# Each norm joined to the projection stage behind it in a two-layer hybrid block

## The chip, the cores and the metric

One Trainium2 chip, one of its cores. A core has TensorE (PE for its matmuls, PEld for its weight loads), VectorE (DVE), ScalarE (ACT), GpSimd (POOL) and SyncE (SP, which issues DMAs here). The metric is the device time of one execution in microseconds, lower is better; a version stands for the median of its runs.

## The reference, cut to what matters

Two layers, 512 latent tokens and 256 context tokens of width 1024. Each layer has two sublayers, and each begins with a layer norm and a modulation (a scale and a shift per channel), whose result goes at once into a wide projection:

```python
def _ln_plain(x):
    xf = x.astype(jnp.float32)
    mu = jnp.mean(xf, axis=-1, keepdims=True)
    var = jnp.mean(jnp.square(xf - mu), axis=-1, keepdims=True)
    return ((xf - mu) * lax.rsqrt(var + LN_EPS)).astype(x.dtype)

def _modulate(x, shift, scale):
    return _ln_plain(x) * (1.0 + scale) + shift
...
        cache, ctx_mix = _ctx_mixer(_modulate(xc, mod_c[0], mod_c[1]), lp, lam, lam_init, not last)
        lat_mix = _latent_mixer(_modulate(x, mod[0], mod[1]), lp, lam, lam_init, cache, cos, sin)
        x = _layernorm(alpha * x + mod[2] * lat_mix, ln1_g[i], ln1_b[i])
        x = _layernorm(alpha * x + mod[5] * _conv_ffn(_modulate(x, mod[3], mod[4]), lp), ln2_g[i], ln2_b[i])
```

The mixers multiply by `w_in` (the recurrent branch's 15 column tiles of it come first in the kernel), `_conv_ffn` multiplies by `ffn_up` (44 column tiles). The last layer's second sublayer works on the 512 latent tokens alone.

## The kernel before

The program is a row of stages. Each is one `stage(nc)` (L108): a block in which each engine runs its own list of instructions in order, with semaphores between them, and at whose end all engines meet at a barrier (L118, L122 in the rows) before the next stage's first instruction of any engine, DMAs included. So a stage cannot load its weights while the one before it runs.

`norm` (L300) is such a stage, and runs four times: before `rwkv_inputs` (L413) and before `ffn` (L1802) in each of the two layers. It works on `nt` token tiles of 128 tokens, 6 of them in the first three norms and 4 in the last. DVE takes the statistics (L318, L322), ACT the square root (L350), DVE the reciprocal and then the normalised tokens `xn`, one `tensor_scalar` for each token tile (L330). Then come eight channel tiles j of 128 channels: TensorE transposes `xn` into PSUM, `nt` transposes for a j (L344), ACT scales and shifts them into one of three slots of `h_f32` (L356), POOL rounds the slot to the fp32r number `h_hi` (L363), and DVE takes the rest, `h_lo` (L334). ACT waits for the `h_lo` three tiles back before it fills a slot again.

A projection, `fm_product` (L396), makes one column tile of 128 outputs for all tokens: for each of the 8 channel tiles k, three products, `w_hi` by `h_hi`, `w_hi` by `h_lo` and `w_lo` by `h_hi`. With 768 tokens each of them is two matmuls (512 and 256 columns), so that a product of one column tile has 48 matmuls; with 512 tokens 24. Its weights come by one DMA of 512 KB (`load_weights`, L379), are rounded by ACT (`split_hi`, L387), and the rest is taken by POOL (`split_lo`, L393). Three raw slots and two split slots hold them: the split for column tile n waits until product n-2 is done. In `rwkv_inputs` ACT copies a finished product out (L575), in `ffn` it does at L1834.

The order is the one written out by hand in these functions; no scheduler changes it.

## Time and profile before

| | us |
|---|---|
| median of 3 runs | 4311.81 (4307.54 to 4319.73) |
| the profiled execution | 4310.86 |
| its span | 4308.5 |
| PE busy | 3610.2 (84% of the span) |
| DVE, ACT, POOL busy | 1549.0, 968.3, 1032.3 |
| granted TensorE clock, mean | 0.928 |

The page has one section that bears on this change, the costliest groups, where the matmuls at L402 (these projections) show a wait for POOL's `w_lo`. The rest is in the trace itself: the list of waits, the timeline around a norm (each row: start, length, engine, line, operation, out<-in, form, count, and in brackets the idle time before it with what ended it), and the windows view, whose columns are the stretch and its length, then the busy time of PE, PEld, DVE, ACT and POOL in it, each with its count (or of one engine alone), the granted clock, the DMA share and GB/s. Clock 0.50 is 1.2 GHz and 1.00 is 2.4 GHz. SPq is SP's queue; a DMA row there is the issue, not the transfer.

### The profile page before, as it was taken

The numbers are of one execution on the slowest core, as the hardware profiler recorded it, in microseconds if no ns is written. First come the engines' busy times: TensorE is split into PE (matmuls) and PEld (weight loads), VectorE is DVE, ScalarE is ACT, GpSimd is POOL, SyncE is SP. The second block draws the span as 40 slices with busy tenths as digits, with TensorE's granted clock in tenths as the row PEclk, the third lists the DMA queues.
The fourth block names the chain that finished last, engine by engine and source line by source line (L and its number), as shares of the span: only waits on it lengthen the run. The fifth ranks groups of instructions, "written<-read, shape, count | busy, mean of one in ns | idle before, by whom it ended". The sixth has DMA issues, their size and how long they took to land. (4 is left out here: it accounts for less than half of the span.)

```text
span 4308.5 us, 80797 instructions
## 1 busy us (share of the span) xinstructions
PE 3610.2 (84%) x36124; PEld 2680.1 (62%) x36124; DVE 1549.0 (36%) x2266; ACT 968.3 (22%) x1743; POOL 1032.3 (24%) x633
## 2 busy tenths in 40 slices
PE   4979999996587888699999497999996687669987
PEld 3658888885355663588734276888774355438843
DVE  2243443332576153311201524444542672331102
ACT  2322212211255120222200142222221342203300
POOL 1222222223232110222200222232232331214401
PEclk8989999998799999799999798999998898879998
DMA  5643333322111231122153054333432102313321
GB/s 196 219 154 105 101 110 101 105 77 109 38 45 46 75 98 78 54 64 64 42 183 138 31 159 132 90 101 108 118 100 86 54 30 94 121 59 93 98 98 39
DMA packets 432706, 410.71 MB, mean 95 GB/s; under 512 B 14244, under 2 KB 367706, under 8 KB 425450
## 3 DMA queue, kind: packets, MB, share of 16 engines
q1 hardware_dynamic: 430778, 396.77, 29.3%
q10 hardware_dynamic: 1584, 8.78, 0.5%
q8 instruction: 285, 4.67, 0.5%
q14 instruction: 59, 0.48, 0.0%
HBM read 325.15 MB, written 80.35 MB: 94 GB/s over the span
## 5 line engine op out<-in xcount | busy, mean ns | idle before, releaser
L799 PE MATMUL ps<-I-280_h_hi,I-1976_w_hi 128*128 128x256 f32 (+1 forms) x832 | 298.4, 359 | 26.9 <-POOL I-1977_w_lo L393 16.0
L799 PE MATMUL ps<-I-280_h_hi,I-1977_w_lo 128*128 128x256 f32 (+1 forms) x832 | 282.2, 339 | 0.1
L799 PE MATMUL ps<-I-281_h_lo,I-1976_w_hi 128*128 128x256 f32 (+1 forms) x832 | 282.1, 339 | 0.0
L1917 PE MATMUL ps<-I-21320_w_down,I-18160_hf 128*128 128x512 f32 x528 | 234.0, 599 | 9.2 <-DMA I-21320_w_down<-in_ffn_down 9.2
L799 PE MATMUL ps<-I-22069_h_hi,I-23484_w_hi 128*128 128x512 f32 (+1 forms) x544 | 215.3, 396 | 19.8 <-POOL I-23485_w_lo L393 14.2
L799 PE MATMUL ps<-I-22070_h_lo,I-23484_w_hi 128*128 128x512 f32 (+1 forms) x544 | 202.5, 372 | 0.5 <-issue 0.5
L799 PE MATMUL ps<-I-22069_h_hi,I-23485_w_lo 128*128 128x512 f32 (+1 forms) x544 | 202.7, 373 | 0.0
L402 PE MATMUL ps<-I-18161_h_hi,I-18370_w_hi 128*128 128x512 f32 x704 | 180.2, 337 | 15.8 <-POOL I-18371_w_lo L393 15.8
L1917 PEld LDWEIGHTS ps<-I-21320_w_down,I-18160_hf 128*128 128x128 f32 x528 | 99.2, 191 | 143.2 <-issue 133.2
L778 POOL CAST I-1976_w_hi<-I-1975_w_raw 128x1024 fp32r<-128x1024 f32 x52 | 56.3, 1082 | 545.7 <-PE ps L799 530.4
L799 PEld LDWEIGHTS ps<-I-280_h_hi,I-1976_w_hi 128*128 128x128 f32 x832 | 157.2, 189 | 43.9 <-POOL I-1977_w_lo L393 16.8
L402 PE MATMUL ps<-I-18162_h_lo,I-18370_w_hi 128*128 128x512 f32 x704 | 180.0, 337 | 0.0
L402 PE MATMUL ps<-I-18161_h_hi,I-18371_w_lo 128*128 128x512 f32 x704 | 179.9, 337 | 0.0
L799 PEld LDWEIGHTS ps<-I-281_h_lo,I-1976_w_hi 128*128 128x128 f32 x832 | 157.9, 190 | 19.2 <-issue 5.0
L799 PEld LDWEIGHTS ps<-I-280_h_hi,I-1977_w_lo 128*128 128x128 f32 x832 | 157.4, 189 | 19.1 <-issue 0.3
L393 POOL TENSOR_TENSOR I-18371_w_lo<-I-18369_w_raw,I-18370_w_hi 128x1024 fp32r<-128x1024 f32 x44 | 105.7, 2403 | 260.5 <-ACT I-18370_w_hi L387 260.5
L778 POOL CAST I-23484_w_hi<-I-23483_w_raw 128x1024 fp32r<-128x1024 f32 x52 | 60.1, 1155 | 444.6 <-PE ps L799 419.1
L1917 PE MATMUL ps<-I-39044_w_down,I-37054_hf 128*128 128x512 f32 x352 | 153.6, 599 | 9.2 <-DMA I-39044_w_down<-in_ffn_down 9.2
L402 PE MATMUL ps<-I-37055_h_hi,I-37230_w_hi 128*128 128x512 f32 x352 | 138.1, 392 | 13.8 <-POOL I-37231_w_lo L393 13.8
L393 POOL TENSOR_TENSOR I-37231_w_lo<-I-37229_w_raw,I-37230_w_hi 128x1024 fp32r<-128x1024 f32 x44 | 105.6, 2401 | 138.2 <-ACT I-37230_w_hi L387 138.2
L402 PE MATMUL ps<-I-37056_h_lo,I-37230_w_hi 128*128 128x512 f32 x352 | 137.8, 392 | 0.0
L402 PE MATMUL ps<-I-37055_h_hi,I-37231_w_lo 128*128 128x512 f32 x352 | 137.7, 391 | 0.0
(837 smaller groups left out, 8202.8 us busy)
## 6 DMA issues: line engine op xcount, KB each, us to landing
I-1975_w_raw<-in_w_in SPq DMA_DIRECT2D x52, 512.0 KB, 5.6
I-23483_w_raw<-in_w_in SPq DMA_DIRECT2D x52, 512.0 KB, 5.1
I-21324_ada_w<-in_ada_w SPq DMA_DIRECT2D x24, 1024.0 KB, 4.9
I-18369_w_raw<-in_ffn_up SPq DMA_DIRECT2D x44, 512.0 KB, 3.9
I-37229_w_raw<-in_ffn_up SPq DMA_DIRECT2D x44, 512.0 KB, 3.8
proj_d<-I-1978_result SPq DMA_DIRECT2D x52, 384.0 KB, 2.8
I-502_ada_w<-in_ada_w SPq DMA_DIRECT2D x16, 1024.0 KB, 5.8
I-21320_w_down<-in_ffn_down SPq DMA_DIRECT2D x22, 512.0 KB, 5.9
```

The costliest lines, as they stand in the source:

```text
L393: eng.tensor_tensor(rings[2][:, n % n_split, 0:kt, :], rings[0][:, n % n_raw, 0:kt, :], rings[1][:, n % n_split, 0:kt, :].bitcast(F32), AL ...
L402: m = pe.matmul(dst[:, at:at + n], w[wi][:, k, :], a[ai][:, k, at:at + n], start=k == 0 and i == 0, stop=k == kt - 1 and i == 2)
L778: pool.tensor_copy(rings[1][:, s % 2, :, :], rings[0][:, s % 3, :, :]).then_inc(sem("w_hi"), 1)
L799: m = pe.matmul(bank(6 + i % 2, n_c), w[:, k, :], hv[:, k, c0:c0 + n_c], start=k == 0 and v == 0, stop=k == KT - 1 and v == 2)
L1917: m = pe.matmul(bank(t), hf[:, g * KG + k, t * P:(t + 1) * P], ring[:, i % SL, k, :], start=g == 0 and k == 0, stop=g == NG - 1 and k == K ...
```

## The change

`norm` is no stage of its own any more. It is called inside the block of `rwkv_inputs` or `ffn` and lays its instructions ahead of theirs on each engine, so that the barrier between the two is gone; SP has no part in the norm, and its first instruction in the block is the load of the first weights. Three things move with it.

First, the weights of column tile 0 are split by ACT ahead of the square root and by POOL ahead of the eight casts; column tiles 1 and on follow behind the norm. Second, the product of column tile 0 waits for `h_lo` tile by tile (`n_lo`), not for the whole norm; its result lies in PSUM banks 0 and 1, and the transposes have three pairs of banks, not four, so that they wait for ACT one tile sooner. Third, one in three of the `xn` tiles goes to ACT, with a bias that a new small DVE instruction makes from mean and reciprocal (`neg_mean`); DVE has 4 of 6 tiles, or 3 of 4. The buffers `xn` and `h_f32` share memory with ones that the stage fills later. The number of matmuls is the same.

```diff
-            with ExitStack() as sc, stage(nc) as (block, sem):
...
+        def norm(sc, block, sem, l, i_shift, i_scale, nt, h, xn, hf, rings):
...
+            by_dve = [t for t in range(nt) if t % 3 != 2]
+            by_act = [t for t in range(nt) if t % 3 == 2]
...
+                dve.wait_ge(sem("n_rstd"), 1)
+                dve.scalar_tensor_tensor(nb[:, 0:nt], mv[:, 0:nt, 0], -1.0, rs[:, 0:nt], ALU.mult, ALU.mult).then_inc(sem("n_nb"), 1)
+                for t in by_dve:
+                    dve.tensor_scalar(xn[:, t, :], x[:, t, :], mv[:, t, 0:1], rs[:, t:t + 1],
+                                      ALU.subtract, ALU.mult).then_inc(sem("n_xn"), 1)
...
+                pe.wait_ge(sem("n_xn"), len(by_dve))
+                pe.wait_ge(sem("n_xa"), len(by_act))
+                for j in range(KT):
+                    if j >= 3:
+                        pe.wait_ge(sem("n_h"), j - 2)
+                    for t in range(nt):
+                        m = pe.transpose(bank(2 + 2 * (j % 3), P, t * P), xn[:, t, j * P:(j + 1) * P], ident[:, :])
...
+                split_hi(act, sem, rings, 0)
+                act.wait_ge(sem("n_var"), 1)
+                act.activation(rs[:, 0:nt], rs[:, 0:nt], ACT.Sqrt).then_inc(sem("n_std"), 1)
+                act.wait_ge(sem("n_nb"), 1)
+                for t in by_act:
+                    act.activation(xn[:, t, :], x[:, t, :], ACT.Identity, bias=nb[:, t:t + 1], scale=rs[:, t:t + 1]).then_inc(sem("n_xa"), 1)
...
+                split_lo(pool, sem, rings, 0)
+                for j in range(KT):
+                    pool.wait_ge(sem("n_h"), j + 1)
+                    pool.tensor_copy(h[0][:, j, 0:n_tok], hf[:, j % 3, 0:n_tok]).then_inc(sem("n_hi"), 1)
...
+                        if s == 1:
+                            pe.wait_ge(sem("n_h"), KT)
                         if s >= 4:
                             pe.wait_ge(sem("hf"), s // 2 - 1)
-                        fm_product(pe, p_of(s), slot(rings, s), h, range(KT), KT, seqs).then_inc(sem("w_used"), 1)
+                        for k in range(KT):
+                            if s == 0:
+                                pe.wait_ge(sem("n_lo"), k + 1)
+                            m = fm_product(pe, p_of(s), slot(rings, s), h, (k,), KT, seqs)
+                        m.then_inc(sem("w_used"), 1)
...
-                    for s in range(3):
+                    for s in range(1, 3):
                         split_hi(act, sem, rings, s)
...
-                    for s in range(2 * FT):
+                    for s in range(1, 2 * FT):
                         split_lo(pool, sem, rings, s)
-                    norm(l, 0, 1, NT, h)
-                    norm(l, 3, 4, LT if last else NT, h)
```

In `rwkv_inputs` the product is cut in the same way, and its first `split_hi` and `split_lo` move too.

Three places in the order of the instructions show this. The first is POOL at the first norm, before (`I-284_h_f` is a slot of `h_f32`, `w_raw`, `w_hi` and `w_lo` are the weights, L118 to L122 the barrier):

```order
L359 UNCONDITIONAL_BRANCH
L363 CAST I-280_h_hi<-I-284_h_f 128x768 x8
L118 UNCONDITIONAL_BRANCH
L121 ISA
L592 UNCONDITIONAL_BRANCH
L393 ISA
L393 TENSOR_TENSOR I-501_w_lo<-I-499_w_raw,I-500_w_hi 128x1024 x15
```

and in the change (the slots of `h_f32` are now `rv_raw`):

```order
L409 UNCONDITIONAL_BRANCH
L328 ISA
L328 TENSOR_TENSOR I-295_w_lo<-I-293_w_raw,I-294_w_hi 128x1024
L414 CAST I-280_h_hi<-I-286_rv_raw 128x768 x8
L608 UNCONDITIONAL_BRANCH
L328 TENSOR_TENSOR I-295_w_lo<-I-293_w_raw,I-294_w_hi 128x1024 x14
```

One subtraction for the weights has moved ahead of the casts, and 14 stand behind them with no barrier between. The second place is ACT at the last norm, the one of 4 token tiles, in the change:

```order
L393 UNCONDITIONAL_BRANCH
L322 ACTIVATE I-37007_w_hi<-I-37006_w_raw 128x1024
L397 ACTIVATE I-37013_rstd<-I-37013_rstd 128x4
L400 ACTIVATE I-37002_hf<-I-49_x,I-37014_neg_mean,I-37013_rstd 128x1024
L406 ACTIVATE I-37010_h_f<-ps,I-64_mod 128x512 x8
L1853 UNCONDITIONAL_BRANCH
L322 ACTIVATE I-37007_w_hi<-I-37006_w_raw 128x1024 x2
```

The rounding of the first weights now stands ahead of the square root (L397), one `xn` tile (L400) behind it, and the rounding for column tile 1 comes right after the last of the eight tiles. The third is TensorE at the first norm, in the change:

```order
L390 MATMUL ps<-I-50_ident,I-283_k_and_kk 128x128 x48
L503 UNCONDITIONAL_BRANCH
L337 MATMUL ps<-I-280_h_hi,I-294_w_hi 128x512
L337 MATMUL ps<-I-280_h_hi,I-294_w_hi 128x256
L337 MATMUL ps<-I-281_h_lo,I-294_w_hi 128x512
```

against before:

```order
L344 MATMUL ps<-I-50_ident,I-283_xn 128x128 x48
L118 UNCONDITIONAL_BRANCH
L495 UNCONDITIONAL_BRANCH
L402 MATMUL ps<-I-280_h_hi,I-500_w_hi 128x512
L402 MATMUL ps<-I-280_h_hi,I-500_w_hi 128x256
```

All 48 transposes still stand ahead of the first product; what is gone between the two is the barrier.

## Rows read from the trace of the kernel before

**Rows 1.** List of waits of PE from 40 to 260 us: waiter, releaser, us in total, times, longest.

```profile
PE ps L402 <- POOL I-501_w_lo L393: 17.0, 1, 17.0
```

**Rows 2.** Timeline from the first norm to the end of the first product.

```profile
41.09 1.28 ACT L350 ACT_TABLE_LOAD   x1 [1.97 <-PEq L122]
41.13 7.22 DVE L318 BATCH_NORM_STATS2 I-285_stats<-I-49_x 128x6 f32<-128x512 f32 x12 [0.86 <-PEq L122]
...
49.52 4.43 DVE L330 TENSOR_SCALAR I-283_xn<-I-49_x,I-286_mean_var,I-287_rstd 128x1024 f32<-128x1024 f32 x6
54.01 7.78 PE L344 MATMUL ps<-I-50_ident,I-283_xn 128*128 128x128 f32 x48 [14.18 <-DVE I-283_xn L330]
...
65.77 1.23 ACT L356 ACTIVATE I-284_h_f<-ps,I-63_mod 128x512 f32<-128x512 f32 x2 [0.30 <-DVE I-281_h_lo L334]
67.06 0.83 POOL L363 CAST I-280_h_hi<-I-284_h_f 128x768 fp32r<-128x768 f32 x1 [0.70 <-ACT I-284_h_f L356]
68.62 0.94 DVE L334 TENSOR_TENSOR I-281_h_lo<-I-284_h_f,I-280_h_hi 128x768 fp32r<-128x768 f32 x1
70.72 0.37 SPq L379 DMA_DIRECT2D I-499_w_raw<-in_w_in  x1
...
75.22 1.06 ACT L387 ACTIVATE I-500_w_hi<-I-499_w_raw 128x1024 fp32r<-128x1024 f32 x1 [8.22 <-DMA I-499_w_raw<-in_w_in]
...
76.36 2.34 POOL L393 TENSOR_TENSOR I-501_w_lo<-I-499_w_raw,I-500_w_hi 128x1024 fp32r<-128x1024 f32 x1 [8.47 <-ACT I-500_w_hi L387]
...
78.75 1.00 PE L402 MATMUL ps<-I-280_h_hi,I-500_w_hi 128*128 128x512 f32 x2 [16.96 <-POOL I-501_w_lo L393]
...
89.25 0.90 ACT L575 ACTIVATE I-489_wa_raw<-ps,I-57_mu_own 128x768 f32<-128x768 f32 x1 [6.37 <-PE ps L402]
```

**Rows 3.** Windows view: the first product behind each of the four norms.

```profile
78.75:89.20 10.45, 10.45 (x52) 8.88 (x56) 0.00 (x0) 1.06 (x1) 2.40 (x1) 0.81 1.00 334
1770.05:1781.25 11.20, 11.20 (x49) 9.69 (x50) 0.00 (x0) 0.00 (x0) 2.28 (x1) 0.75 0.32 94
2481.18:2491.90 10.72, 10.72 (x49) 9.30 (x50) 0.00 (x0) 1.06 (x1) 2.37 (x1) 0.79 0.43 118
3870.07:3878.10 8.03, 8.03 (x25) 6.42 (x26) 0.00 (x0) 0.00 (x0) 2.26 (x1) 0.70 0.45 131
```

**Rows 4.** Timeline: last h_lo and end of product 0, second and third norm.

```profile
1760.57 0.94 DVE L334 TENSOR_TENSOR I-18162_h_lo<-I-18165_h_f,I-18161_h_hi 128x768 fp32r<-128x768 f32 x1
...
1781.33 1.06 ACT L387 ACTIVATE I-18370_w_hi<-I-18369_w_raw 128x1024 fp32r<-128x1024 f32 x1 [11.95 <-PE ps L402]
...
2472.04 0.94 DVE L334 TENSOR_TENSOR I-22070_h_lo<-I-22073_h_f,I-22069_h_hi 128x768 fp32r<-128x768 f32 x1
...
2491.94 0.90 ACT L575 ACTIVATE I-22278_wa_raw<-ps,I-58_mu_own 128x768 f32<-128x768 f32 x1 [9.63 <-PE ps L402]
```

**Rows 5.** Timeline of the fourth norm, of 4 token tiles.

```profile
3841.82 4.85 DVE L318 BATCH_NORM_STATS2 I-37060_stats<-I-49_x 128x6 f32<-128x512 f32 x8 [2.93 <-PEq L122]
...
3847.47 0.18 DVE L327 RECIPROCAL I-37062_rstd<-I-37062_rstd 128x4 f32<-128x4 f32 x1 [0.27 <-ACT I-37062_rstd L350]
...
3860.94 0.69 DVE L334 TENSOR_TENSOR I-37056_h_lo<-I-37059_h_f,I-37055_h_hi 128x512 fp32r<-128x512 f32 x1 [0.51 <-POOL I-37055_h_hi L363]
...
3866.53 1.06 ACT L387 ACTIVATE I-37230_w_hi<-I-37229_w_raw 128x1024 fp32r<-128x1024 f32 x1 [6.84 <-DMA I-37229_w_raw<-in_ffn_up]
...
3878.15 1.06 ACT L387 ACTIVATE I-37230_w_hi<-I-37229_w_raw 128x1024 fp32r<-128x1024 f32 x1 [8.75 <-PE ps L402]
```

**Rows 6.** Timeline: the same DVE instruction alone, and beside a POOL instruction.

```profile
1696.37 0.81 DVE L1780 TENSOR_SCALAR I-49_x<-I-49_x,I-17981_mean_var,I-17982_rstd 128x1024 f32<-128x1024 f32 x1
...
1726.00 2.34 POOL L1794 TENSOR_TENSOR I-49_x<-I-49_x,I-17866_ln_b 128x1024 f32<-128x1024 f32 x1 [11.38 <-DVE I-49_x L1782]
1726.03 2.86 DVE L1780 TENSOR_SCALAR I-49_x<-I-49_x,I-17981_mean_var,I-17982_rstd 128x1024 f32<-128x1024 f32 x1
```

**Rows 7.** Windows view, from 2.2 us behind the first norm's transposes.

```profile
64.00:70.00 6.00, 0.00 (x0) 0.00 (x0) 5.56 (x5) 2.46 (x4) 2.48 (x3) 0.64 0.00 0
```

More of the change, by code:

```diff
@@ L420, in rwkv_inputs @@
             with ExitStack() as s2, stage(nc) as (block, sem):
-                kf = sb(s2, "k_raw", [P, CTILES, TOK])
+                kfk = sb(s2, "k_and_kk", [P, 2, CTILES, TOK])
+                kf, kk = kfk[:, 0], kfk[:, 1]
                 wa = sb(s2, "wa_raw", [P, 2, TOK])
@@ L431, in rwkv_inputs @@
                 rings = weight_rings(s2, 3, 2)
+                xn = kfk[:, :, :, :].rearrange("p a t n -> p (a t n)").rearrange("p (t d) -> p t d", t=NT)
+                norm(s2, block, sem, l, 0, 1, NT, h, xn, rv, rings)
                 src = A["w_in"][l].rearrange("(k p) n -> p k n", p=P)
@@ L533, in _ @@
                         pe.wait_ge(sem("w_lo"), n + 1)
+                        if n == 1:
+                            pe.wait_ge(sem("n_h"), KT)
                         if n >= 2:
                             pe.wait_ge(sem("shifted"), n - 1)
-                        fm_product(pe, p_of(n), slot(rings, n), h, range(4), KT, seqs(mains[n]))
+                        for k in range(4):
+                            if n == 0:
+                                pe.wait_ge(sem("n_lo"), k + 1)
+                            fm_product(pe, p_of(n), slot(rings, n), h, (k,), KT, seqs(mains[n]))
                         beside(2 * n)
-                        fm_product(pe, p_of(n), slot(rings, n), h, range(4, KT), KT, seqs(mains[n])).then_inc(sem("w_used"), 1)
+                        for k in range(4, KT):
+                            if n == 0:
+                                pe.wait_ge(sem("n_lo"), k + 1)
+                            m = fm_product(pe, p_of(n), slot(rings, n), h, (k,), KT, seqs(mains[n]))
+                        m.then_inc(sem("w_used"), 1)
                         beside(2 * n + 1)
@@ L593, in _ @@
                 def _(pool):
-                    for n in range(N):
+                    for n in range(1, N):
                         split_lo(pool, sem, rings, n)
@@ L1809, in ffn @@
                 cv = sb(s2, "conv", [P, 2, TOK])
+                xn = hf[:, FT - KT:FT, :].rearrange("p j n -> p (j n)").rearrange("p (t d) -> p t d", d=D_MODEL)
+                h3 = sb(s2, "h_f32", [P, 3, TOK])
+                norm(s2, block, sem, l, 3, 4, nt, h, xn, h3, rings)
                 src = A["ffn_up"][l].rearrange("(k p) n -> p k n", p=P)
```

102 lines of the change are left out of this document (43 added, 59 removed).

## The prediction

> **What bounds the kernel now.** I first read the list of waits of TensorE for the stretch of the first norm and the projections behind it. Its longest entry is one wait of 17.0 us for POOL's `w_lo` [rows 1]. The timeline shows what lies in it [rows 2]. The transposes end at 54.01 + 7.78 = 61.8. The last `h_lo` ends at 68.62 + 0.94 = 69.56. Only then, behind the barrier, does SP issue the load of the first weights (70.72); they are there at 75.22, ACT rounds them for 1.06 us, POOL takes the rest for 2.34 us, and the first matmul starts at 78.75. So 9.2 us pass between the end of the norm and the first product, in which ACT and POOL together have 3.4 us of work, and all of it serves a load that depends on nothing the norm makes. The product of column tile 0 then runs from 78.75 until ACT may copy it out at 89.25.
>
> That pattern occurs four times. In the second and third norm the last `h_lo` ends at 1761.51 and 2472.98, and product 0 has ended at 1781.3 and 2491.9 [rows 4]; in the fourth it is 3861.63 and 3878.1 [rows 3, 5]. The windows view says what product 0 is made of: 10.45 us at a mean granted clock of 0.81 [rows 3]. 10.45 x 0.81 = 8.46 us is what it needs at 2.4 GHz, so 2.0 us are lost because the clock stood at 1.2 GHz when it began. The others give 8.40, 8.47 and 5.62 us, and losses of 2.8, 2.25 and 2.4; the four losses come to 9.4 us. One channel tile of eight thus costs 1.06 us at 2.4 GHz, and 0.70 us with 512 tokens. Behind product 0 TensorE is the bound of these stages: [rows 1] gives the wait for `w_lo` as one single time up to 260 us, so whatever product 0 ends earlier, the stage ends earlier.
>
> **The change part by part.** I work in the times of the trace of before, and ask when product 0 ends.
>
> The gap. The load is now issued when the block starts, near 41.1. In [rows 2] it took 75.22 - 70.72 = 4.5 us, so it lands at 45.6; ACT rounds until 46.7, then loads its table (1.28 us, until 48.0). The statistics end at 41.13 + 7.22 = 48.35 and the root is wanted about 0.7 us before `xn` starts at 49.52, so ACT is free 0.8 us before. POOL's subtraction runs from 46.8 to 49.1, and it had nothing to do then. SP's other loads and the three large ones of `ada_w` come earlier too, and wait for nothing new. The cost of these moved steps in the three norms with 6 token tiles is taken as nothing; the DVE statistics cover it. If POOL and the statistics hinder one another, it costs up to 2.86 - 0.81 = 2.05 us a norm, what a DVE instruction lost beside POOL in [rows 6]; below nothing it cannot be, as the norm is not made shorter by it. No row shows statistics beside POOL, so both ends stay in the range, and I take nothing because the subtraction is over by 49.1, before the long `xn` instructions begin.
>
> `xn`. Six instructions take 4.43 us on DVE [rows 2], 0.74 each. Four take 2.95, and the new small one costs about as much as the reciprocal, 0.18 us [rows 5], with its semaphore 0.22. ACT's two tiles are the size of a weight rounding, 1.06 us each: 2.1 us, hidden beside DVE's 2.95. Gain 4.43 - 2.95 - 0.22 = 1.25 us in each of the first three norms.
>
> The fourth norm has less cover. Its statistics take 4.85 us from 3841.82 [rows 5]. The weights land at 3841.8 + 4.5 = 3846.3, ACT has rounded them at 3847.4, and POOL works from 3847.5 to 3849.8. DVE's reciprocal is done at 3847.65, so the small instruction and three `xn` tiles fall right onto POOL. [rows 6] show the price: the same form on DVE takes 0.81 us alone and 2.86 us when it starts 0.03 us behind a POOL instruction of 2.34, so it stands still until POOL ends. I let DVE wait until 3849.8: 3849.8 + 0.22 + 3 x 0.74 = 3852.25, where before it was done at about 3847.68 + 4 x 0.74 = 3850.65. This norm loses 1.6 us at `xn`; the bounds are that and a gain of 0.5.
>
> Product 0, fed tile by tile. TensorE runs in order, so it starts only behind all transposes. Those wait for ACT one tile sooner, but the last ACT tile began at 65.77, 4 us behind the transposes' end, so the eighth transpose has room. From 61.8 seven tiles of 1.06 us need 7.4 us, until 69.2; the seventh `h_lo` ends at 68.62, where the eighth begins [rows 2], so tile seven ends at 69.2 to 69.7 and TensorE keeps up with DVE. The eighth decides. ACT is done with its last tile at 65.77 + 1.23 = 67.0, rounds column tile 1 until 68.1, and POOL, whose last cast ended at 67.89, asks for its subtraction at about 68.15, while DVE is in the seventh `h_lo`. When that ends at 68.62, POOL has been waiting longest. I let it go first, as in [rows 6]: the eighth `h_lo` starts 2.34 us late. Product 0 ends at 68.62 + 2.34 + 0.94 + 0.1 + 1.06 = 73.06 (0.1 for two semaphores), less 1.25: 71.8. Product 1 finds its `w_lo` ready at 68.62 + 2.34 = 70.96, less 1.25.
>
> The Trainium skill (SBUF — State Buffer, section "Who interferes with whom") says that DVE and GpSimd share a pair of ports as a lock: a DVE instruction with two SBUF inputs, or in a two-port mode, and a GpSimd instruction that reads SBUF shut each other out for the whole length, and whichever issues first goes first; one with a single input outside those modes is not hindered. By that rule the tail goes to POOL and the statistics pay nothing, which is the sum below; were nothing shared, the sum would be 4.1 us at the tails and 2.1 us at the fourth `xn` better. [rows 6] agree with the lock, with 2.86 us against 0.81.
>
> The sum, as the end of product 0 before less the end now:
> - first norm: 89.2 - 71.8 = 17.4
> - second: 1781.3 - (1760.57 + 4.44 - 1.25 = 1763.75) = 17.5
> - third: 2491.9 - (2472.04 + 4.44 - 1.25 = 2475.25) = 16.7
> - fourth: 3878.1 - (3860.94 + 2.34 + 0.69 + 0.1 + 0.70 + 1.6 = 3866.4) = 11.7
>
> Together 63.3 us. The jump from the norm's list to the stage's on each engine is new and not in the trace; a barrier with two jumps and SP's first issue takes 70.72 - 69.56 = 1.16 us, so one jump costs 0 to 1.16. On TensorE it is hidden, since it comes seven tiles before the deciding one; on ACT it would only turn the tail over, which is the first rival. The profiled execution was 4310.86, 1 us from the median 4311.81: 4310.86 - 63.3 = 4247.6.
>
> **The rivals.**
> (a) DVE goes first at the tails. If ACT's jump costs more than 0.5 us, POOL asks behind 68.62 and the eighth `h_lo` is not held. Then `w_lo` of column tile 1 decides: 69.56 + 2.34 + 0.05 = 71.95 for product 1's start, against 73.06. That is 1.1 us better, 3 x 1.1 + 0.8 = 4.1 in all: 4243.5. Against it, the margin of 0.5 us is most of what a barrier costs.
> (b) The clock is not kept. [rows 7] show it at a mean of 0.64 from 64 to 70 us, which is 2.4 GHz for 0.28 x 6 = 1.7 us, until 65.7: it fell 3.9 us behind the last transpose. The idle time I leave TensorE before tile eight is 73.06 - 1.06 - 69.7 = 2.3 us, shorter. A clock at 1.2 GHz during product 0 alone is nearly free (61.8 + 11.2 = 73.0, no later than DVE allows). But if it falls at the tail, product 1 pays what product 0 paid before, 9.4 us in all: 4257.
> (c) The weights' steps hinder the first three norms as well: 3 x 2.05 = 6.2 us, 4253.8.
> (d) The change doesn't overlap as it says, and product 0 runs wholly behind the last `h_lo`: it loses seven tiles each, 3 x 7.4 + 4.9 = 27.1 us, 4274.7. The order of the instructions speaks against it.
> (e) Slower than before. ACT now waits for the first weights ahead of the square root, and everything in the norm hangs on that root. Each microsecond that the load takes beyond about 5.3 us (4.5 and the 0.8 of slack) delays the norm by one. To lose 13 us overall each load would have to be late by (63.3 + 13) / 4 = 19 us, so to take 24 us against the 4.5 of [rows 2]. No row speaks for that.
>
> **How the numbers follow.** Forecast 0.52, (a) 0.16, (b) 0.14, (c) 0.09, (d) 0.04; 0.04 for a gain that is partly given back in the stages, most of it still faster, and 0.01 for (e). The range runs from (a), 4243.5, and from (b), 4257, each with some 4 us more for the jump, the fourth norm and the spread of three runs: 4239 to 4261. It leaves out (d), (e) and the rest, about 0.1, and a mixture of (b) and (c). A measurement of this kernel can tell about 0.3%, 13 us, from no change: faster by more 0.97, within 0.02, slower 0.01.
>
> **What would show it.** In the trace of the changed kernel the first `w_raw` load is issued with the statistics, `w_lo` ends before `xn` starts, and TensorE's wait behind the transposes is no longer 17 us but several short ones for DVE's `h_lo`, the last near 2.3 us. At the tail a POOL subtraction of 2.34 us stands between the seventh and eighth `h_lo`. `xn` ends 1.25 us sooner in three norms and later in the fourth. I am wrong if the clock is at 0.5 in product 1, if ACT's table load or root comes late, or if the stages behind product 0 have grown.

## The result and the profile after the change

The changed kernel takes 4256.28 us (median of 4 runs, 4247.08 to 4261.71), beside 4312.68 for the kernel before (4 runs, 4307.54 to 4319.73). The medians lie 56.4 us apart. The ratio is 0.9863, with a 95% interval of 0.9848 to 0.9878: faster by 1.4%, clear of the noise. The forecast was 4247.6 in a range of 4239 to 4261. The profiled run took 4255.81 us with a span of 4254.0, where the kernel before had 4310.86 and 4308.5.

First the list of waits of TensorE for the changed kernel, in the stretch of [rows 1] (waiter, releaser, us in total, times, longest):

```profile
PE ps L390 <- DVE I-283_k_and_kk L375: 12.8, 1, 12.8
...
PE ps L337 <- DVE I-281_h_lo L379: 1.7, 1, 1.7
```

The 17.0 us for `w_lo` are gone. What is left is the wait ahead of the transposes (L390) for the `xn` tiles (their buffer bears the name `k_and_kk` here), which was there before too (14.18 in [rows 2]), and 1.7 us for one `h_lo`. The timeline of the first norm answers to [rows 2] (start, length, engine and line, operation, in brackets the idle time before it and its releaser):

```profile
41.26 0.37 SPq L314 DMA_DIRECT2D I-293_w_raw<-in_w_in  x1
41.30 7.22 DVE L362 BATCH_NORM_STATS2 I-296_stats<-I-49_x 128x6 f32<-128x512 f32 x12 [0.86 <-PEq L122]
...
45.38 1.06 ACT L322 ACTIVATE I-294_w_hi<-I-293_w_raw 128x1024 fp32r<-128x1024 f32 x1 [6.09 <-DMA I-293_w_raw<-in_w_in]
...
46.46 1.28 ACT L397 ACT_TABLE_LOAD   x1
46.52 2.34 POOL L328 TENSOR_TENSOR I-295_w_lo<-I-293_w_raw,I-294_w_hi 128x1024 fp32r<-128x1024 f32 x1 [45.60 <-ACT I-294_w_hi L322]
...
49.23 0.21 ACT L397 ACTIVATE I-298_rstd<-I-298_rstd 128x6 f32<-128x6 f32 x1 [1.49 <-DVE I-298_rstd L369]
...
61.27 0.60 PE L337 MATMUL ps<-I-280_h_hi,I-294_w_hi 128*128 128x512 f32 x2
...
66.83 2.90 POOL L328 TENSOR_TENSOR I-295_w_lo<-I-293_w_raw,I-294_w_hi 128x1024 fp32r<-128x1024 f32 x1
...
70.60 0.62 PE L337 MATMUL ps<-I-280_h_hi,I-294_w_hi 128*128 128x512 f32 x2 [1.71 <-DVE I-281_h_lo L379]
...
71.96 0.90 ACT L591 ACTIVATE I-284_wa_raw<-ps,I-57_mu_own 128x768 f32<-128x768 f32 x1 [5.21 <-PE ps L337]
```

The load is issued with the statistics and both splits are over by 48.9, before `xn` starts. ACT stands idle for 1.49 us ahead of the square root, so the weights' steps cost the norm nothing. The first matmul of product 0 starts at 61.27, right behind the transposes, and product 0 is copied out at 71.96 instead of 89.25. The windows view gives product 0 at each of the four places, as [rows 3] did (window, its length, busy us of PE, PEld, DVE, ACT and POOL, then the granted clock):

```profile
61.20:72.00 10.80, 9.09 (x55) 7.52 (x57) 9.35 (x6) 4.69 (x8) 6.32 (x5) 1.00 0.00 0
1733.50:1744.40 10.90, 9.77 (x56) 8.31 (x55) 8.39 (x5) 5.03 (x9) 5.43 (x4) 1.00 0.17 47
2433.50:2444.30 10.80, 9.09 (x53) 7.72 (x52) 9.32 (x6) 4.73 (x8) 6.30 (x5) 1.00 0.08 22
3815.00:3823.40 8.40, 6.57 (x29) 5.12 (x28) 5.53 (x4) 3.41 (x5) 5.24 (x5) 1.00 0.17 49
```

The granted clock is 1.00 (2.4 GHz) at all four, where it was 0.81, 0.75, 0.79 and 0.70. Product 0 is not much shorter than before. Its first seven channel tiles run through right behind the transposes, and ahead of the eighth TensorE waits for the last `h_lo`, 1.71, 1.13, 1.71 and 1.83 us at the four places, where before it ran at 1.2 GHz behind the norm.

**Where the time went.** I cut each execution into five parts: four places, each from the start of a norm's statistics to the start of ACT's copy of product 0 (in the two ffn ACT rounds another column tile ahead of that copy, before and after alike); the first layer's ffn, from its first copy to its last (22 copies, each of two column tiles); and the rest. All are read off the traces, and the parts sum to the span up to rounding.

```
us                         four places                 sum     ffn of layer 0   rest     span
before                     48.1  49.2  47.4  37.3     182.0   348.4            3778.1   4308.5
after                      30.7  31.7  30.6  25.6     118.6   355.1            3780.3   4254.0
```

The four places gained 63.4 us. The first ffn lost 6.7 and the rest 2.2, which leaves 54.5.

The 6.7 us are not a wait. The windows view has TensorE busy all through the stage and the granted clock at 1.00, in the kernel before and then in the changed one:

```profile
1790.00:2130.00 340.00, 340.00 (x1963) 297.39 (x1962) 61.06 (x100) 76.82 (x82) 98.59 (x41) 1.00 0.21 59
```

```profile
1750.00:2095.00 345.00, 345.00 (x1954) 299.22 (x1954) 61.07 (x100) 77.20 (x82) 98.26 (x41) 1.00 0.20 59
```

But the matmuls take a little longer. The groups by form, first of the kernel before from 1800 to 2130 us, then of the changed one from 1765 to 2095 (busy us, mean ns of one):

```profile
L402 PE MATMUL ps<-I-18161_h_hi,I-18370_w_hi 128*128 128x512 f32 x318 | 125.1, 394 | 0.0
L402 PE MATMUL ps<-I-18162_h_lo,I-18370_w_hi 128*128 128x512 f32 x318 | 125.1, 394 | 0.0
...
L402 PE MATMUL ps<-I-18162_h_lo,I-18370_w_hi 128*128 128x256 f32 x317 | 87.8, 277 | 0.0
```

```profile
L337 PE MATMUL ps<-I-18144_h_lo,I-18147_w_hi 128*128 128x512 f32 x312 | 125.8, 403 | 0.0
L337 PE MATMUL ps<-I-18143_h_hi,I-18148_w_lo 128*128 128x512 f32 x312 | 124.2, 398 | 0.0
L337 PE MATMUL ps<-I-18143_h_hi,I-18147_w_hi 128*128 128x512 f32 x311 | 122.9, 395 | 0.0
L337 PE MATMUL ps<-I-18144_h_lo,I-18147_w_hi 128*128 128x256 f32 x312 | 88.6, 284 | 0.0
```

The lengths overlap, since a matmul starts before the one ahead of it ends. A 128x512 matmul with `h_lo` takes 403 ns instead of 394, one of 256 columns 284 instead of 277; the other two products have 398 and 395 with 512 columns. So the loss is not spread evenly: one of the three products of each channel tile takes most of it. In the second execution of this kernel (again, below) that one was `h_hi` by `w_hi`. The six matmuls of a channel tile start 1040 ns after those of the last one in before (1043 and 1037 in turn), and 1060 in after, from the second product to the last without a drift. I call these the 1040 and the 1060 pace. From the first to the last of ACT's copies there are 336 channel tiles: 336 x 0.02 = 6.7 us.

### The profile page after: what moved, and what is told of

Its sections match the earlier page's. It is cut to its first block and busy times, and to the rows that moved or that the text cites. A ratio compares the mean times of both kernels' runs of the same rounds, so it can differ in the third digit from the quotient of the medians.

```text
span 4254.0 us, 80709 instructions
## 1 busy us (share of the span) xinstructions
PE 3614.4 (85%) x36124; PEld 2680.1 (63%) x36124; DVE 1555.2 (37%) x2263; ACT 976.0 (23%) x1750; POOL 1032.5 (24%) x633
## 5 line engine op out<-in xcount | busy, mean ns | idle before, releaser
L815 PE MATMUL ps<-I-280_h_hi,I-1958_w_hi 128*128 128x256 f32 (+1 forms) x832 | 299.6, 360 | 20.5 <-POOL I-1959_w_lo L328 15.0
L815 PE MATMUL ps<-I-281_h_lo,I-1958_w_hi 128*128 128x256 f32 (+1 forms) x832 | 283.2, 340 | 3.2 <-issue 3.2
L815 PE MATMUL ps<-I-280_h_hi,I-1959_w_lo 128*128 128x256 f32 (+1 forms) x832 | 283.4, 341 | 0.0
L1942 PE MATMUL ps<-I-21286_w_down,I-18142_hf 128*128 128x512 f32 x528 | 234.1, 600 | 9.1 <-DMA I-21286_w_down<-in_ffn_down 9.1
L815 PE MATMUL ps<-I-22035_h_hi,I-23432_w_hi 128*128 128x512 f32 (+1 forms) x544 | 215.8, 397 | 19.1 <-POOL I-23433_w_lo L328 15.2
L815 PE MATMUL ps<-I-22036_h_lo,I-23432_w_hi 128*128 128x512 f32 (+1 forms) x544 | 202.9, 373 | 0.0
L815 PE MATMUL ps<-I-22035_h_hi,I-23433_w_lo 128*128 128x512 f32 (+1 forms) x544 | 202.8, 373 | 0.0
L337 PE MATMUL ps<-I-18144_h_lo,I-18147_w_hi 128*128 128x512 f32 x704 | 184.7, 343 | 0.0
L337 PE MATMUL ps<-I-18143_h_hi,I-18147_w_hi 128*128 128x512 f32 x704 | 181.0, 338 | 1.1 <-DVE I-18144_h_lo L379 1.1
L337 PE MATMUL ps<-I-18143_h_hi,I-18148_w_lo 128*128 128x512 f32 x704 | 180.8, 338 | 0.0
L337 PE MATMUL ps<-I-37003_h_hi,I-37007_w_hi 128*128 128x512 f32 x352 | 137.2, 390 | 1.8 <-DVE I-37004_h_lo L379 1.8
L337 PE MATMUL ps<-I-37003_h_hi,I-37008_w_lo 128*128 128x512 f32 x352 | 137.0, 389 | 0.0
```

Of the source, the lines that this page charges most:

```text
L337: m = pe.matmul(dst[:, at:at + n], w[wi][:, k, :], a[ai][:, k, at:at + n], start=k == 0 and i == 0, stop=k == kt - 1 and i == 2)
L815: m = pe.matmul(bank(6 + i % 2, n_c), w[:, k, :], hv[:, k, c0:c0 + n_c], start=k == 0 and v == 0, stop=k == KT - 1 and v == 2)
L1942: m = pe.matmul(bank(t), hf[:, g * KG + k, t * P:(t + 1) * P], ring[:, i % SL, k, :], start=g == 0 and k == 0, stop=g == NG - 1 and k == K ...
```

## The experiments

Each is compared with the unchanged second run of the changed kernel or with the kernel before, part by part. All stand in one table, in us; "pace" is that of a channel tile in the first ffn, whose copies span 348.4 us at 1040 and 355.1 at 1060.

```
                           four places                 sum     pace, ns   rest     span
before                     48.1  49.2  47.4  37.3     182.0    1040      3778.1   4308.5
after                      30.7  31.7  30.6  25.6     118.6    1060      3780.3   4254.0
again                      30.7  31.7  30.7  25.0     117.9    1060      3781.6   4254.6
no_tile_feed               40.4  40.3  40.1  31.4     152.2    1040      3767.7   4268.3
late_split                 38.5  39.9  39.7  30.1     148.1    1040      3776.3   4272.8
second_split_early         29.2  30.1  29.2  23.2     111.7    1040      3785.2   4245.3
second_split_early_again   29.2  30.1  28.7  23.7     111.7    1040      3777.8   4237.9
merge_alone                41.3  42.8  41.2  30.8     156.1    1060      3778.7   4289.9
xn_all_dve                 32.3  33.1  32.0  26.0     123.4    1040      3774.2   4246.0
xn_all_dve_again           32.0  33.1  32.9  25.5     123.6    1060      3780.9   4259.6
late_load                  37.9  38.4  37.7  30.5     144.6    1060      3778.6   4278.3
hold_in_product0           29.3  31.0  29.2  23.3     112.8    1060      3779.6   4247.5
hold_again                 28.7  30.9  29.2  23.7     112.5    1060      3772.9   4240.5
hold_before_product1       28.7  30.3  29.2  23.7     111.9    1060      3782.9   4249.9
```

The places repeat within 0.9 us each and 0.7 in their sum; the rest goes from 3767.7 to 3785.2. No experiment edits anything in it (in two executions a late fall of the clock reaches into it, as told under (b) below). Most of the spread lies in the two layers' long stretches from product 0 to the norm ahead of the ffn (1635.8 to 1646.0 and 1346.4 to 1356.4 us). So a mechanism is read at its places, and a whole time alone settles nothing under some 10 us.

**again.** The changed kernel, nothing edited.

> The changed kernel once more. The four places gained 63.3 us in its first trace, as in the sum of the prediction, but the span fell by 54.5 only: 6.8 us went in the first layer's feed-forward projection, where a column tile took 16.91 / 2 us where before it took 16.59 / 2, with no wait of TensorE. Theory A (the rate of these matmuls varies from one execution to the next, with no tie to the change): the pace there differs from 16.91 for a pair in some of the traces of this call. Theory B (the change slows them): 16.91 again in each kernel that keeps its instructions. Time: 4250 to 4260.

4253.74 us, ratio 0.9848 (0.9833 to 0.9863), the places within 0.7 us in sum, and the same 1060 pace, which either theory allows.

**no_tile_feed.** Product 0 waits for all eight `h_lo`:

```
-                                pe.wait_ge(sem("n_lo"), k + 1)
+                                pe.wait_ge(sem("n_lo"), KT)
```

> Product 0 of each projection waits for all eight h_lo tiles, not tile by tile; all else as in the changed kernel. Theory: product 0 then starts at the last h_lo (70.55 us at the first norm) behind 9 us of idle TensorE, so that the clock has fallen, and takes as long as before the change, 10.45, 11.2, 10.7 and 8.0 us: it ends 9.2, 9.8, 9.4 and 7.0 us later than in the changed kernel, 35.4 us in all (4256 + 35 = 4291). Rival 1 (the clock holds): 7.4, 7.4, 7.4, 4.9, so 27 us. Rival 2 (the feed is worth nothing, since the early weights are what counts): within 5 us of the changed kernel.

4285.43 us, ratio 0.9924 (0.9907 to 0.994). The places lose 33.6 us against after, near the 35.4 of the theory, and the clock was lost: the windows view grants 0.50 over the first 3 us of product 0 in the second and third norm.

**late_split.** The split of the first weights stands behind the norm's own instructions on ACT and on POOL:

```
             def _(act):
-                split_hi(act, sem, rings, 0)
...
                     m.then_inc(sem("n_h"), 1)
+                split_hi(act, sem, rings, 0)
...
             def _(pool):
-                split_lo(pool, sem, rings, 0)
...
+                split_lo(pool, sem, rings, 0)
```

> The split of column tile 0's weights goes behind the norm's instructions on ACT and POOL; its load stays early, the feed tile by tile stays. Theory: POOL ends it at 69.75 at the first norm, TensorE has been idle for 8 us, product 0 runs cold and ends near 80.2 where the changed kernel has 71.9: 8.4, 8.9 and 8.5 us later in the first three norms; in the fourth 4.3, because POOL no longer stands in the way of DVE's small instructions there (2.2 us). 30 us in all, 4286. Rival (the load alone is what had to be early, 5.6 us of the 9.2 us gap): about 3.4 us a norm, 14 in all.

4272.77 us, ratio 0.9892 (0.9877 to 0.9906), and 29.5 us lost at the places, with 30 expected. The whole time came out 13 us under the 4286 expected: the profiled execution had the 1040 pace (6.7 us) and 4 us less in the rest than after. The timeline of its second norm shows the way:

```profile
1745.86 5.92 POOL L328 TENSOR_TENSOR I-18148_w_lo<-I-18146_w_raw,I-18147_w_hi 128x1024 fp32r<-128x1024 f32 x2
1748.78 0.50 PEld L337 LDWEIGHTS ps<-I-18143_h_hi,I-18147_w_hi 128*128 128x128 f32 x2 [7.78 <-POOL I-18148_w_lo L328]
1748.79 1.01 PE L337 MATMUL ps<-I-18143_h_hi,I-18147_w_hi 128*128 128x512 f32 x2 [7.55 <-POOL I-18148_w_lo L328]
```

POOL makes the first `w_lo` only behind its last cast, TensorE waits 7.55 us for it, and the clock is lost again: over 1745 to 1754 us the windows view grants 0.56, and two matmuls take 1.01 us where the changed kernel's take 0.60. Feeding tile by tile brings little without the early split, since product 0 needs `w_lo` in its first channel tile.

**merge_alone.** Both edits above, and all of `xn` on DVE; what stays is the single block with the early load.

> What is left of the change when its three parts are taken out: the norm still shares its block with the projection and the weights are still loaded at its start, but they are split behind the norm, product 0 waits for all of h_lo, and DVE makes all xn tiles. Theory: the barrier and the load (5.7 us of the 9.2 us gap) are gone, the split of 3.4 us is half hidden by the last h_lo tiles, product 0 runs cold as before: 6.9, 6.1, 5.8 and 6.2 us sooner than in the kernel before, 25 in all, 4290. Rival (the parts are not additive, each removes the same idle time): 40 us or more sooner.

4290.08 us, ratio 0.9922 (0.99 to 0.9944). The places gain 26.0 us on before: the load of 4.5 us and the barrier are hidden. Of the other 156.1 - 118.6 = 37.5 us, `xn` is 4.9 if it is worth here what xn_all_dve shows in the changed kernel (no run tests that), so tile feed and early split together are 32.6, not 33.6 + 29.5. With neither of them the places would come to 156.1 - 4.9 = 151.2; with the feed alone (late_split) they have 148.1, with the early split alone (no_tile_feed) 152.2. The two are one edit in two halves.

**xn_all_dve.** All token tiles of the norm on DVE (a list `by_dve` of all tiles and an empty `by_act`, and without the small instruction L373 for ACT's bias).

> The changed kernel with all xn tiles on DVE and without the small neg_mean instruction. Theory: product 0 ends 1.25 us later in the first three norms and 0.5 us later in the fourth, 4.3 us in all: 4259. Rival (ACT's share is worth nothing, since the transposes wait for something else): within 1 us at each place. If the pace of the second norm's projection goes back from 1060 to 1040 ns for a channel tile, 6.9 us come back and the time is 4252; this theory says nothing on that.

4263.07 us, ratio 0.9865 (0.984 to 0.989); 4.8 us lost at the places, and 5.0 in its second execution, with 4.3 expected.

**late_load.** SP issues the first weights only when the statistics are done:

```
+            if late and n == 0:
+                sp.wait_ge(sem("n_var"), 1)
```

> SP holds back the load of column tile 0 until DVE has the variances, about 8 us into the block (5.5 in the fourth norm); all else as in the changed kernel. This tests the rival in which ACT's wait for the weights ahead of the square root holds the norm. Theory: the root is late by what the load is late beyond the slack of 1.5 to 2.7 us seen in the changed trace: 6.4 us at the first norm (4.2 landing, 1.06 rounding, 1.28 table), 5.3 at the second and third, and POOL's subtraction then falls onto DVE's xn and costs up to 2 us more: 8, 7, 7 and 5 us, 27 in all, 4283. Other theory (ACT's place in the order is harmless, since TensorE waits for h_lo anyway): under 5 us.

4285.11 us, ratio 0.9922 (0.9906 to 0.9939); 25.9 us lost at the places, with 27 expected. Its first norm's timeline:

```profile
49.43 0.37 SPq L316 DMA_DIRECT2D I-293_w_raw<-in_w_in  x1
...
53.80 1.06 ACT L324 ACTIVATE I-294_w_hi<-I-293_w_raw 128x1024 fp32r<-128x1024 f32 x1 [14.31 <-DMA I-293_w_raw<-in_w_in]
...
54.88 1.28 ACT L399 ACT_TABLE_LOAD   x1
...
56.17 0.21 ACT L399 ACTIVATE I-298_rstd<-I-298_rstd 128x6 f32<-128x6 f32 x1
56.41 0.19 DVE L373 RECIPROCAL I-298_rstd<-I-298_rstd 128x6 f32<-128x6 f32 x1 [7.01 <-ACT I-298_rstd L399]
56.64 0.66 DVE L375 SCALAR_TENSOR_TENSOR I-299_neg_mean<-I-297_mean_var,I-298_rstd 128x6 f32<-128x6 f32 x1
```

The statistics start at 41.51 here. Counted from them, the load was issued 8.0 us later than in after and took 0.2 us more to be used; less the slack of 1.5 us that makes 6.7, and the root came 6.7 us later (14.66 us behind the start of the statistics against 7.93). The small instruction of L375 took 0.5 us more beside POOL, and this place lost 7.2. So at this place a late load costs what exceeds the slack of 1.5 us, one for one, as the rival on the slower side had it. Even a load 8 us later in three norms and 5.4 in the fourth leaves the kernel faster than before.

**second_split_early.** The split of column tile 1 is taken away from the tail of the norm: ACT does its half behind its `xn` tiles, POOL its half ahead of the casts, behind DVE's `xn`:

```
                 split_lo(pool, sem, rings, 0)
+                pool.wait_ge(sem("n_xn"), len(by_dve))
+                split_lo(pool, sem, rings, 1)
```

(ACT gets `split_hi(act, sem, rings, 1)` behind its `xn` loop, and the stage's own loops begin one column tile later.)

> Column tile 1 is also split ahead of the casts: by ACT behind its xn tiles, by POOL as soon as DVE has finished xn, while both engines wait for the first transposes. Theory: nothing stands between the seventh and the eighth h_lo any more, so that DVE's last one takes 0.94 us, not 3.1, and product 0 ends 1.9, 1.4, 1.9 and 1.8 us sooner than in the changed kernel; product 1 finds its weights ready. 7 us faster, 4249. Rival (the subtraction of 2.34 us merely moves the hold-up to the first cast): within 2 us of the changed kernel, and the first h_hi cast starts later by up to 2 us.

> second_split_early unchanged, a second time, in more rounds: its ratio to the kernel before was 0.9829 and that of after 0.9848 beside it, 6.4 to 8 us apart, of which 6.8 was counted at the four places (1.3 to 2.3 us at each) and 6.9 more would lie in the first ffn if its pace stays at 16.59 us for two products. Both would make 13.7 us under after, about 4240 to 4243; the four places alone make about 4247. Expected 4245, ratio 0.983 (0.981 to 0.985), pace 16.59, the places at 29.2, 30.1, 29.2 and 23.2 us.

4245.64 us, ratio 0.9829 (0.9814 to 0.9843); the second time 4250.28 and 0.9851 (0.983 to 0.9872), 5 us above the 4245 expected. The places gain 6.9 us on after in either execution. The timelines say why; first the tail of the second norm in after, then where the same split went in second_split_early:

```profile
1735.72 6.18 DVE L379 TENSOR_TENSOR I-18144_h_lo<-I-18150_h_f,I-18143_h_hi 128x768 fp32r<-128x768 f32 x3
...
1737.18 0.84 POOL L414 CAST I-18143_h_hi<-I-18150_h_f 128x768 fp32r<-128x768 f32 x1 [0.67 <-ACT I-18150_h_f L406]
1738.15 2.93 POOL L328 TENSOR_TENSOR I-18148_w_lo<-I-18146_w_raw,I-18147_w_hi 128x1024 fp32r<-128x1024 f32 x1
...
1741.95 0.62 PE L337 MATMUL ps<-I-18143_h_hi,I-18147_w_hi 128*128 128x512 f32 x2 [1.13 <-DVE I-18144_h_lo L379]
```

```profile
1725.58 2.36 POOL L328 TENSOR_TENSOR I-18149_w_lo<-I-18147_w_raw,I-18148_w_hi 128x1024 fp32r<-128x1024 f32 x1 [4.21 <-ACT I-18148_w_hi L322]
1726.60 2.51 ACT L407 ACTIVATE I-18151_h_f<-ps,I-63_mod 128x512 f32<-128x512 f32 x4 [1.17 <-PE ps L390]
1727.90 0.82 POOL L417 CAST I-18144_h_hi<-I-18151_h_f 128x768 fp32r<-128x768 f32 x1
```

In the one it stands between DVE and its last `h_lo`; in the other it fills the time in which the first transposes run and POOL has nothing to cast. By whole times it lies 8 us under again, beside which it was measured, with intervals that overlap, and the second time its ratio is no better than that of again (0.9851 and 0.9848). So whole times do not show that it is better; the places do, by 6.9 us twice.

With the tail gone TensorE decides these places. Product 0 runs through, and what is left to differ is a wait in the transposes for ACT to empty one of the three pairs of banks: of 1.0 to 1.1 us where the place has 29.2, and absent where it has 28.7 (first and third norm of these two and the hold kernels; one with 0.86 us has 29.3). In after such a wait (1.08 us, second norm) costs nothing, since DVE decides there.

**The pace: hold_in_product0, hold_again, hold_before_product1, xn_all_dve_again.** The changed kernel stops TensorE for 1.1 us inside product 0 (L337 above), and runs at 1060 from there; before and second_split_early have no such stop and run at 1040. Theory A: the stop makes the pace. The hold kernels are second_split_early with three more DVE instructions and a wait for them on TensorE, in layer 0's ffn alone, in hold_in_product0 (and hold_again, the same kernel) ahead of the eighth channel tile:

```
+                            if s == 0 and k == KT - 1 and not last:
+                                pe.wait_ge(sem("hold"), 1)
```

In hold_before_product1 the wait stands under `if s == 1`, ahead of product 1.

> The kernel with the second split early, and in the first layer's feed-forward stage three more DVE instructions of 0.6 us behind the last h_lo, for which TensorE waits ahead of the eighth channel tile of product 0 (they change nothing in the data). In the changed kernel TensorE stood still for 1.1 us at this place and then needed 1060 ns for each channel tile until the end of the stage, 43 products; with the second split early it did not stand still and needed 1040. Theory (a stop of TensorE inside product 0 sets the slower pace): 1060 again in this stage, 7 us more, 4252. Rival (the pace comes from something else, such as when product 1 begins against POOL or ACT): 1040, 4246.

> hold_in_product0 unchanged, a second time. If the pace of the first ffn's matmuls belongs to the program (the instants at which TensorE starts and stops in it), it is 16.91 us for two products again; if it is drawn at each execution, it may be 16.59. after and its repeat both had 16.91, which is one pair; this is a second. Four places 29.3, 31.0, 29.2, 23.3 us as the first time, each within 0.3.

> The kernel of hold_in_product0 with its wait moved: in the ffn of layer 0 TensorE waits for the three extra 0.6 us VectorE instructions (which multiply three h_lo tiles by 1.0 and change no data) ahead of product 1 instead of ahead of the last channel tile of product 0. The question is the pace of that stage's matmuls, which was 16.59 us for each two products in before and 16.91 in after. Theory A (a stop inside product 0 brings the slow pace) expects 16.59 here, since product 0 runs through and the stop lies between two products; theory B (the pace is picked anew at any restart, by something that no row shows) allows either. merge_alone, with 16.91 and no stop inside product 0, already speaks against A. The four places should stay at 29.2, 30 to 31, 29.2 and 23.2 us from the statistics to the copy out of product 0; the span is 4240 to 4250 with 16.59 and 7 us more with 16.91.

> xn_all_dve unchanged, a second time: it has a stop inside product 0 of the first ffn and still ran at 16.59 us for two products. A pace that belongs to the program gives 16.59 again; a drawn one gives 16.91 at about even odds, and then no cause is to be looked for in the kernel's text. Four places 32.3, 33.1, 32.1 and 26.1 us, each within 0.3.

hold_in_product0 had the 1060 pace (4249.29 us), as A wants; so had hold_again (4242.25) and hold_before_product1 (4251.68), and merge_alone without any stop inside product 0. The intervals between the last matmuls (`w_lo` by `h_hi`, 256 columns) of successive channel tiles overturn A. The first seven lie inside product 0, a bar, then come those of product 1 (ns, in the first ffn):

```
before                 1920 1900 1047 1042 1038 1042 1038 | 1042 1038 ...
after                  1040 1040 1040 1040 1040 1040 2465 | 1060 1060 ...
xn_all_dve             1040 1040 1040 1040 1040 1116 3037 | 1040 1040 ...
xn_all_dve_again       1038 1042 1038 1042 1038 1126 3065 | 1060 1060 ...
late_load              1060 1060 1060 1060 1060 1060 2326 | 1060 1060 ...
hold_in_product0       1060 1060 1060 1060 1060 1060 1718 | 1060 1060 ...
hold_before_product1   1060 1060 1060 1060 1060 1060 1060 | 1060 1060 ...
second_split_early     1040 1040 1040 1040 1040 1040 1040 | 1040 1040 ...
```

The places of the two repeats missed their expected 0.3 us at times: hold_again had 28.7 for 29.3 in the first norm and 23.7 for 23.3 in the fourth, xn_all_dve_again 32.9 for 32.1 in the third (its clock fell there) and 25.5 for 26.1 in the fourth.

In the hold kernels TensorE had the 1060 pace from the second tile on, before it ever came to the added wait. The wait was also short: 0.4 us in hold_in_product0 and hold_again, and in hold_before_product1 it never held TensorE. There the three added instructions (L1898) were over at 1744.69, and ACT, which waits for the end of product 0, went on only at 1745.57:

```profile
1743.19 1.50 DVE L1898 TENSOR_SCALAR I-18151_h_f<-I-18151_h_f 128x768 f32<-128x768 f32 x3
1745.57 1.06 ACT L322 ACTIVATE I-18148_w_hi<-I-18147_w_raw 128x1024 fp32r<-128x1024 f32 x1 [4.98 <-PE ps L337]
```

So that run tests no stop between products. And xn_all_dve is one program with both paces in two executions. Their first full matmuls behind the stop stand side by side in the timelines, first the execution with 1040, then that with 1060:

```profile
1745.59 0.61 PE L337 MATMUL ps<-I-18138_h_hi,I-18142_w_hi 128*128 128x512 f32 x2 [1.72 <-DVE I-18139_h_lo L378]
1746.04 0.52 PE L337 MATMUL ps<-I-18139_h_lo,I-18142_w_hi 128*128 128x512 f32 x2
```

```profile
1745.58 0.62 PE L337 MATMUL ps<-I-18138_h_hi,I-18142_w_hi 128*128 128x512 f32 x2 [1.73 <-DVE I-18139_h_lo L378]
1746.04 0.53 PE L337 MATMUL ps<-I-18139_h_lo,I-18142_w_hi 128*128 128x512 f32 x2
```

The POOL split and the `h_lo` ahead of them start within 0.02 us of each other in the two. So the kernel's text alone does not settle the pace; it is there when TensorE starts and can change when it stops. The two executions of xn_all_dve were on two chips. Each of these chips showed both paces, among different kernels, so the chip alone does not settle it either; one program with both paces on one chip was not seen. Of 14 profiled executions nine had 1040 in product 0 once the clock was at 1.00, and five 1060. Of the nine, the five that never stopped inside product 0 stayed at 1040 (before, no_tile_feed, late_split, and second_split_early twice); of the four that stopped (after, again, xn_all_dve twice), three went over to 1060. None went from 1060 to 1040. That a stop inside product 0 makes 1060 likelier fits these counts but is not shown by them, and what picks the pace stays open.

## Why the prediction came out as it did

**The sum held at every place.** Predicted 17.4, 17.5, 16.7 and 11.7 us; measured 17.5, 17.5, 16.7 and 11.7 in after, and 17.5, 17.6, 16.7 and 12.3 in again. Its terms, one by one:
- *The gap at no cost*: right. ACT idles 1.49 us ahead of the root in the first norm (0.8 was worked out) and 2.5 to 2.7 in the others, where no table load stands.
- *`xn`*: the last `xn` tile ends at 49.78 + 2.97 = 52.75, 11.45 us behind the start of the statistics, where it was 12.82: 1.37 us gained, 1.25 predicted. xn_all_dve prices it from the other side at 4.8 to 5.0 us in all, with 4.3 expected.
- *The fourth norm*: the 1.6 us lost were 1.5, but by another instruction than I named. I had the small instruction for ACT's bias (L373) and three `xn` tiles run onto POOL; it caught the one before, L369, which adds the epsilon to the variance. Its four executions:

```profile
L369 DVE TENSOR_SCALAR I-298_rstd<-I-297_mean_var x1: 172/172/172, 49.0 to 49.0; 128x6 f32<-128x6 f32 x1
L369 DVE TENSOR_SCALAR I-18153_rstd<-I-18152_mean_var x1: 374/374/374, 1720.3 to 1720.3; 128x6 f32<-128x6 f32 x1
L369 DVE TENSOR_SCALAR I-22053_rstd<-I-22052_mean_var x1: 170/170/170, 2421.3 to 2421.3; 128x6 f32<-128x6 f32 x1
L369 DVE TENSOR_SCALAR I-37013_rstd<-I-37012_mean_var x1: 2347/2347/2347, 3803.0 to 3803.0; 128x4 f32<-128x4 f32 x1
```

  Beside POOL's subtraction (3802.95, 2.34 us) an instruction of four columns took 2.35 us instead of 0.17. The end was the same because DVE stands until POOL ends, whichever instruction it has. In again POOL came 0.04 us behind L369, which took 0.17 us, and the instruction that I had named was the one that stood:

```profile
3803.77 2.34 POOL L328 TENSOR_TENSOR I-37008_w_lo<-I-37006_w_raw,I-37007_w_hi 128x1024 fp32r<-128x1024 f32 x1 [5.75 <-ACT I-37007_w_hi L322]
3804.39 1.74 DVE L373 SCALAR_TENSOR_TENSOR I-37014_neg_mean<-I-37012_mean_var,I-37013_rstd 128x4 f32<-128x4 f32 x1
```

  There this norm's transposes began 0.9 us later than in before, not 1.5: which instruction is caught, and 0.6 us of this term, hang on less than 0.1 us in POOL's start.
- *The tail*: POOL's split went ahead of the eighth `h_lo` at all four places, as forecast. The longest `h_lo` took 3126, 3143, 3125 and 2839 ns, with 958 and 677 alone. The first one ended at 70.55; the sum has 71.9 - 1.25 = 70.65. second_split_early, which takes just this collision away, gave 6.9 us, with 7 expected.
- *Room for the eighth transpose*: not so, without effect. The transposes took 61.51 - 52.81 = 8.7 us in the first norm where they took 7.8, and in the second they waited 1.08 us for ACT; the last `h_lo` came later than that all the same.

**The rivals.** (a) is excluded by the rows on the tail. (b) did not happen in the profiled executions of the changed kernel: the clock is 1.00 in all four windows of after, and stays there in product 1. But its mechanism is real, and nearer than a wait of 7.55 us (late_split, 0.56). TensorE stops for 1.7 to 1.8 us at such a tail 17 times in the 14 traces. Behind 14 of these stops the clock stayed at 1.00; behind three it stood at 0.50 within 1.6 us: at the third norm of xn_all_dve_again and at the first and fourth of late_load. First the stop in xn_all_dve_again and the 3 us behind it, then the 3 us behind the same stop, also of 1.73 us, in xn_all_dve:

```profile
2446.72 0.91 PE L337 MATMUL ps<-I-22025_h_hi,I-22039_w_hi 128*128 128x512 f32 x2 [1.73 <-DVE I-22026_h_lo L378]
2447.06:2450.06 3.00, 3.00 (x11) 2.52 (x11) 0.17 (x1) 1.11 (x2) 0.00 (x0) 0.50 0.61 174
```

```profile
2440.45:2443.45 3.00, 3.00 (x19) 2.64 (x18) 1.03 (x2) 1.85 (x2) 0.04 (x1) 1.00 0.62 174
```

That fall cost 0.9 us at the place and 0.6 behind it; in late_load the stages behind the two falls took 2.3 and 1.6 us longer. So the stop at the tail is kept free of cost by a margin that the traces show to fail at times, which is one more reason for second_split_early, where it is gone. (c) is excluded: the statistics beside POOL take what they always took (here the first norm's; POOL's subtraction runs from 46.52 to 48.86, and in before they took 677 to 695 ns).

```profile
L362 DVE BATCH_NORM_STATS2 I-296_stats<-I-49_x x12: 674/676/694, 41.3 to 47.8; 128x6 f32<-128x512 f32 x12
```

By the rule of the Trainium skill (SBUF — State Buffer, section "Who interferes with whom") a DVE instruction with two SBUF inputs or in a two-port mode is shut out by a GpSimd instruction that reads SBUF, and one with a single input outside those modes is not. The trace agrees, with 674 to 694 ns for the statistics and 3126 against 958 for `h_lo`. (d) costs 33.6 us when it is brought about, more than the 27.1 worked out, as TensorE then waits 9.14, 8.45, 9.15 and 6.69 us ahead of product 0 and starts it at a clock of 0.50: the clock was lost too, which (d) left out. (e) has the right slope and no cause.

**What did not hold** is the step "whatever product 0 ends earlier, the stage ends earlier", which the sum took as nothing lost behind product 0. The median came out 8.7 us above the forecast, and the profiled run 8.2 us (4255.81 against 4247.6): 6.7 are the 1060 pace in the first ffn and 2.2 the rest, less 0.1 by which the places came out better and 0.55 that lie around the span (2.36 us before, 1.81 after). In three of the four stages the step held: from the first to the last of ACT's copies `rwkv_inputs` took 165.5 and 130.0 us before and 165.6 and 130.0 after, and the ffn of layer 1 227.5 both times. Only the first ffn grew. The 2.2 us of the rest lie elsewhere, mainly in -3.2 and +3.7 us on the two long stretches from product 0 to the norm ahead of the ffn, and 1.3 behind the last ffn copy. Neither is an effect that the edit can be shown to have. The pace came up in both profiled executions of the changed kernel, but xn_all_dve, one program, had either, and the rest varies by 17 us among kernels that don't touch it. A forecast of this kernel by places can be good to 0.1 to 0.6 us a place, and still miss by some 7 to 9 us. The range covered that, for other reasons (rival (b), four late clocks): that the measured 4256 lies next to the 4257 of (b) is luck.

## What to carry to other kernels

A load and a conversion that depend on nothing in a stage belong at its start, on engines whose own first work waits for another; what limits this is the slack in front of that work, 1.5 us here, and every microsecond beyond it counted in full at the place where it was read. Feeding a product tile by tile only pays when all its other operands are ready too: here the feed alone was worth 3 us, the early split alone nothing (1 us lost), and both together 32.6 us. Place a long POOL instruction where DVE has neither one with two inputs nor a `TENSOR_SCALAR`, and look at which instruction stands next to it, not at its size: four columns waited 2.3 us. And where a trace shows a stop of TensorE that the clock survives, look at a second execution: behind the same stop of 1.73 us it was kept once and lost once.

## What the runs showed of the hardware

- TensorE has, at a granted clock of 1.00 and with no wait in between, two paces for the same stream of matmuls: 1040 and 1060 ns for six (three of 512 and three of 256 columns), each kept from product 1 to the end of the stage, 348 or 355 us. The Trainium skill (TensorE: Matmul & The Clock Gate, section "Wait — 56ns, not 53.3ns?") gives for matmuls back to back one distance from start to start, the columns at 2.4 GHz and some 2.5 ns: by it an estimate for six would be 3 x 768 / 2.4 + 15 = 975 ns. Both paces lie above it; in this stream each matmul has a weight load of its own. In product 0 of `rwkv_inputs` six of the same sizes took 1053 ns, and the ffn of layer 1, with 512 columns in each of three matmuls, ran at 680 ns, both in every execution while the clock was at 1.00.
- The smallest DVE instructions are shut out by POOL as well: `TENSOR_SCALAR` of 128x4 took 2347 ns instead of 170, and `SCALAR_TENSOR_TENSOR` of 128x6 (128x4 in the fourth norm) took 0.66, 2.08, 2.08 and 2.09 us instead of 0.17 in late_load's four norms, where it ran beside POOL's split. A `RECIPROCAL` of 128x4 beside the same split took its usual 0.18 us (again, fourth norm).
- A stop of TensorE of 1.7 to 1.8 us between stretches at a granted clock of 1.00 left the clock there 14 times and was followed by 0.50 three times, in one case behind the same stop of the same program (1.73 us).
